# Query and key projection of a head pair as seven block products, spread expert slots and expert transposes

## The reference

```python
def sb_attend(q, k, v, q_pos, k_pos, bias):
    z = jnp.einsum('bqhe,bkhe->bhqk', q, k) * (HEAD_DIM ** -0.5) + bias
    mask = k_pos[None, :] < q_pos[:, None]
    log_beta = jax.nn.log_sigmoid(z)
    log_rest = jnp.where(mask, jax.nn.log_sigmoid(-z), 0.0)
    tail = lax.cumsum(log_rest, axis=3, reverse=True) - log_rest
    a = jnp.where(mask, jnp.exp(log_beta + tail), 0.0)
    return jnp.einsum('bhqk,bkhe->bqhe', a, v)

# layer 0
qkv = (rmsnorm(xp, g_attn[0]) @ w_qkv_a[0]).reshape(b, s, 3, N_HEADS_A, HEAD_DIM)
o_p = sb_prompt(qkv[:, :, 0], qkv[:, :, 1], qkv[:, :, 2], sb_bias[0])
xp = xp + o_p.reshape(b, s, -1) @ w_o_a[0]

def hmoe(h, ...):           # end of each layer; two experts a token, in one group
    a = jnp.einsum('td,edf->tef', h, w_g)
    u = jnp.einsum('td,edf->tef', h, w_u)
    return jnp.einsum('tef,efd->td', jax.nn.silu(a) * u * comb[:, :, None], w_d)
```

## Time and profile before

| what | before |
|---|---|
| median of 3 runs | 1375.42 us (1375.24 to 1375.64) |
| the profiled execution | 1374.61 us |
| its span | 1372.7 us |
| mean granted clock of TensorE in it | 0.987 |
| TensorE busy | 95% |
| VectorE, ScalarE, GpSimd busy | 46%, 24%, 33% |

### The profile page before, as it was taken

How to read it: one execution, slowest core, us unless ns; L and a number is a source line. 1 busy time by engine, 2 the same in 40 slices (tenths; PEclk the granted TensorE clock), 3 DMA queues, 4 the chain that set the end, 5 groups by cost and what they waited for, 6 DMA issues and landing times. The chain is left out here.

```text
span 1372.7 us, 20982 instructions
## 1 busy us (share of the span) xinstructions
PE 1297.9 (95%) x8732; PEld 919.7 (67%) x8732; DVE 637.2 (46%) x997; ACT 332.1 (24%) x667; POOL 451.9 (33%) x385
## 2 busy tenths in 40 slices
PE   8999999999999998899999999999998989999786
PEld 6787888545566764547868867877845656766453
DVE  3577675623622221164558558558436472121114
ACT  2222322302122221240115005005005312222112
POOL 2233444101011111005876576576450111111101
PEclk9999999999899999999999999999999999999998
DMA  8366534377699999971112012013050899999996
GB/s 312 135 219 220 194 106 174 101 309 299 246 418 418 419 418 420 412 289 51 57 56 94 12 55 94 11 56 96 9 139 2 330 353 419 417 419 419 419 417 259
DMA packets 92768, 318.83 MB, mean 232 GB/s; under 512 B 32969, under 2 KB 45401, under 8 KB 66564
## 3 DMA queue, kind: packets, MB, share of 16 engines
q1 hardware_dynamic: 77956, 279.95, 52.5%
q0 software_dynamic: 13536, 33.29, 6.7%
q10 hardware_dynamic: 1184, 4.26, 0.8%
HBM read 300.19 MB, written 33.28 MB: 243 GB/s over the span
## 5 line engine op out<-in xcount | busy, mean ns | idle before, releaser
L1941 PE MATMUL ps<-slots 128*128 128x384 f32 x768 | 262.0, 495 | 0.9 <-DVE vo L2240 0.6
L1941 PEld LDWEIGHTS ps<-slots 128*128 128x128 f32 x768 | 203.0, 270 | 43.7 <-issue 3.2
L1092 PE MATMUL ps<-slots,oT 128*64 128x256 f32 x1344 | 178.4, 390 | 23.3 <-DMA slots<-in_w_up 18.6
L581 PE MATMUL ps<-xnT_a,wA 128*128 128x260 f32 (+1 forms) x768 | 173.3, 386 | 1.7 <-DVE xnT_a L791 1.4
L1092 PEld LDWEIGHTS ps<-slots,oT 128*64 128x64 f32 x1344 | 121.4, 141 | 74.2 <-issue 26.2
L581 PEld LDWEIGHTS ps<-xnT_a,wA 128*128 128x128 f32 x768 | 145.6, 191 | 27.0 <-issue 5.8
L1604 POOL DMA_INDIRECT y_rows<-ysb,idx x30 | 30.2, 1007 | 361.1 <-DVE ysb L1127 361.1
L1118 DVE TENSOR_TENSOR sg<-sg,ps 64x256 f32<-64x256 f32 x64 | 26.5, 414 | 236.2 <-ACT sg L1115 236.2
L1127 DVE COPY ysb<-ps 64x512 f32<-64x512 f32 x60 | 41.6, 694 | 82.8 <-PE ps L1110 82.8
L1115 ACT ACTIVATE sg<-ps 64x256 f32<-64x256 f32 x64 | 24.4, 381 | 227.5 <-PE ps L1092 227.5
L2178 ACT ACTIVATE slots<-slots,neg 128x128 f32<-128x128 f32 (+1 forms) x192 | 64.1, 417 | 54.8 <-DVE neg L2285 49.3
(11 more groups left out here) (311 smaller groups left out, 2129.5 us busy)
## 6 DMA issues: line engine op xcount, KB each, us to landing
slots<-in_w_gate SPq DMA_DIRECT2D x42, 1024.0 KB, 23.2
slots<-in_w_up SPq DMA_DIRECT2D x42, 1024.0 KB, 26.6
slots<-in_w_down SPq DMA_DIRECT2D x36, 1024.0 KB, 26.1
slots<-in_unit_weights_b SPq DMA_DIRECT2D x12, 1536.0 KB, 7.1
wA<-in_qkv_pairs_a SPq DMA_DIRECT2D x24, 512.0 KB, 4.4
apart<-in_w_down SPq DMA_DIRECT2D x8, 1024.0 KB, 27.8
spare<-in_w_down SPq DMA_DIRECT2D x8, 1024.0 KB, 24.5
apart<-in_w_up SPq DMA_DIRECT2D x6, 1024.0 KB, 27.9
```

The costliest lines, as they stand in the source:

```text
L581: last = nc.tensor.matmul(bank(6 + h)[:, 0:half], wA[:, m, k, :], xnT[:, k, half * h:half * h + half], start=(k == 0), stop=(k == KT - 1))
L1092: last = nc.tensor.matmul(bank(q)[lo:lo + CAP, 0:FE], x[:, k, :], wt[:, k, :], start=(k == 0), stop=(k == KT - 1))
L1941: last = nc.tensor.matmul(bank(i % 2)[:, 0:UW], xT[:, kt, cols], wB[:, g, kt, :], start=(kt == 0), stop=(kt == KT - 1))
```

## The change

**Projection.** Write the 1024 inputs as two halves (weight tiles 0 to 3 and 4 to 7) and the 520 tokens as two halves of 260. Queries and keys of a pair for both token halves are a 2x2 block product of weights (q, k by input half) and tokens (input half by token half). It was eight block products of 4 matmuls; now it is seven, of sums and differences of blocks. GpSimd makes the mixed tokens once (`mix_tokens`, four operations on 1040 columns) and the mixed weights for every pair from 1 on (`mix_weights`, four on 512 columns). The mixed blocks live in `apart` and `wo_hi`, so the output weights 4 to 7 are loaded later. Three of the seven results are used more than once: ScalarE keeps product 1, VectorE adds what stands in the banks to it (`read`). Pair 0 is projected as before.

```diff
+        HK = KT // 2
+        NPROD, NREAD = 7, 5
+        mixed = flat(wo_hi)
...
+                def mixed_part(at, weights, tokens, start, stop):
+                    for k in range(HK):
+                        last = nc.tensor.matmul(bank(at)[:, 0:HALF], weights[:, k, :], tokens[:, k, :],
+                                                start=(start and k == 0), stop=(stop and k == HK - 1), skip_group_check=True)
+                    last.then_inc(s_mp, 1)
...
+                    pe.wait_ge(s_w[0], 16 * n + 16)
+                    pe.wait_ge(s_kve, 4 * n)
+                    mixed_part(7, q[:, 0:HK], x11, True, False)
+                    pe.wait_ge(s_mixw, 4 * n)
+                    pe.wait_ge(s_mixx, 4)
+                    mixed_part(6, mix_w[:, 1], mix_x[1], True, False)
+                    pe.wait_ge(s_ma, a + 1)
+                    mixed_part(7, q[:, HK:KT], x21, False, True)
+                    pe.wait_ge(s_md, d + 1)
+                    mixed_part(6, mix_w[:, 2], mix_x[2], False, False)
+                    pe.wait_ge(s_ma, a + 2)
+                    mixed_part(7, mix_w[:, 0], mix_x[0], True, False)
+                    pe.wait_ge(s_md, d + 2)
+                    pe.wait_ge(s_w[1], 16 * n + 16)
+                    mixed_part(6, kw[:, HK:KT], mix_x[3], False, True)
+                    pe.wait_ge(s_md, d + 3)
+                    mixed_part(7, mix_w[:, 3], x22, False, True)
...
+                def read(n, i, out, kept, at):
+                    dve.wait_ge(s_mp, NPROD * (n - 1) + (2, 4, 5, 6, 7)[i])
...
+                    nc.vector.tensor_tensor(out, kept, bank(at)[:, 0:HALF], ALU.add).then_inc(s_md, 1)
...
+                    nc.gpsimd.tensor_tensor(mix_w[:, 0], kw[:, 0:HK], kw[:, HK:KT], ALU.add).then_inc(s_mixw, 1)
+                    nc.gpsimd.tensor_tensor(mix_w[:, 2], q[:, 0:HK], kw[:, 0:HK], ALU.subtract).then_inc(s_mixw, 1)
...
                         if n < LAST:
-                            sp.wait_ge(s_proj, 6 * n + 2 * m + 2)
+                            if n and m < 2:
+                                sp.wait_ge(s_mixw, 4 * n)
+                                sp.wait_ge(s_mp, NPROD * (n - 1) + (3, 6)[m])
+                            else:
+                                sp.wait_ge(s_proj, in_plain(m, n, 1))
                             load_qkv(m, n + 1)
```

**Rows and transposes.** `iota64` now holds for slot c the place c // 4 + 16 (c mod 4), so the rows of an expert lie at every fourth slot first. The first transpose of a block and the first of each expert's hidden rows, which were products with the identity matrix, are now transposes like the others. Where further blocks are turned (`product`), nothing changes.

```diff
-    put("iota64", np.broadcast_to(np.arange(CAP), (128, CAP)))
+    slot = np.arange(CAP)
+    put("iota64", np.broadcast_to(slot // 4 + 16 * (slot % 4), (128, CAP)))
...
                     for i in range(HALFK):
-                        out, rows = bank(2 + half)[:, 128 * i:128 * i + 128], xs[w][:, HALFK * half + i:D:KT]
-                        if half == 0 and i == 0:
-                            last = nc.tensor.matmul(out, rows, ident, start=True, stop=True)
-                        else:
-                            last = nc.tensor.transpose(out, rows, ident)
+                        last = nc.tensor.transpose(bank(2 + half)[:, 128 * i:128 * i + 128], xs[w][:, HALFK * half + i:D:KT], ident)
...
-                        if product or f == 0:
+                        if product:
                             last = nc.tensor.matmul(out, cols, ident[0:CAP, 0:CAP], start=True, stop=True)
```

More of the change, by code:

```diff
@@ L426, in build, with in_plain @@
         LAST = NPAIR - 1
+        HK = KT // 2
+        NPROD, NREAD = 7, 5
+        mixed = flat(wo_hi)
+        mix_w = mixed[:, 0:4 * HK * 128].rearrange("p (i k c) -> p i k c", i=4, k=HK)
+        first_p, sum_16, sum_167 = [mixed[:, 4 * HK * 128 + HALF * i:4 * HK * 128 + HALF * (i + 1)] for i in range(3)]
+        mix_x = [flat(apart)[:, HK * HALF * i:HK * HALF * (i + 1)].rearrange("p (k m) -> p k m", k=HK) for i in range(3)]
+        mix_x.append(mixed[:, D * NPAIR // 2 - HK * HALF:].rearrange("p (k m) -> p k m", k=HK))
+        def in_plain(m, n, h):
+            return 2 * m + h + 1 if n == 0 else 6 + 2 * (n - 1) + h + 1
         with ExitStack() as ph, nc.Block() as block:
@@ L475, in build @@
                                  "srows_copied_act"))
+            early_sems = [s_mixx, s_mixw, s_mp, s_ma, s_md, s_qp, s_qr, s_qst, s_nb]
+            for early in early_sems:
+                live[-1].remove(early)
             s_w0, s_zero, s_tops = sem("sweights_cleared"), sem("zero_row"), sem("tables_read")
@@ L571, in project @@
                     half = SEQ // 2 if m == 0 else HALF
-                    for h in range(2):
+                    for h in halves:
+                        if n and h == 1:
+                            pe.wait_ge(s_md, NREAD * n)
                         if m == 0 and n == 0 and h == 1:
@@ L586, in turn_kv, with kv_place @@
+                def kv_place(c, n, t):
+                    o = 1536 + NZ if c == 0 and n and t == NT - 1 else 512 * 6 + 128 * t
+                    return ps[0:TILES[t][1], o:o + 128]
                 def turn_kv(c, n):
-                    pe.wait_ge(s_pev, 6 * n + 4 + 2 * c)
+                    if c == 0 and n:
+                        pe.wait_ge(s_md, NREAD * (n - 1) + 4)
+                    else:
+                        pe.wait_ge(s_pev, in_plain(1 + c, n, 1))
                     for t, rows in TILES:
-                        last = nc.tensor.transpose(ps[0:rows, 512 * 6 + 128 * t:512 * 6 + 128 * t + 128],
-                                                   qkvT[:, 1 + c, 128 * t:128 * t + rows], ident)
+                        last = nc.tensor.transpose(kv_place(c, n, t), qkvT[:, 1 + c, 128 * t:128 * t + rows], ident)
@@ L856, in _ @@
                         out_a.add(dve, 0, 1)
+                    else:
+                        read(n + 1, 0, sum_16, first_p, 6)
                     for h in range(2):
+                        if n < LAST and h == 1:
+                            early_keys(n + 1)
+                            late_queries(n + 1)
                         dve.wait_ge(s_msk, 4 * n + 2 * h + 2)
@@ L861, in _ @@
                             nc.vector.tensor_tensor_scan(P, P, keep[:, at:at + width][:, ::-1], 1.0, ALU.mult, ALU.add).then_inc(s_scan, 1)
+                            if n < LAST and h == 0 and lo == 0:
+                                read(n + 1, 1, sum_167, first_p, 6)
+                        if n < LAST and h == 0:
+                            late_keys(n + 1)
                         dve.wait_ge(s_scan, 4 * n + 2 * h + 2)
@@ L935, in next_keys, with mix_tokens, mix_weights @@
                             past(u + 3, 0)
+                def mix_tokens():
+                    b11, b12, b21, b22 = [xnT[:, HK * i:HK * i + HK, HALF * j:HALF * j + HALF] for i in range(2) for j in range(2)]
+                    for out, one, other, after in ((0, b12, b11, 0), (2, b22, b12, 0), (1, b22, mix_x[0], 1), (3, b21, mix_x[1], 3)):
+                        if after:
+                            pool.wait_ge(s_mixx, after)
+                        nc.gpsimd.tensor_tensor(mix_x[out], one, other, ALU.subtract).then_inc(s_mixx, 1)
+                def mix_weights(n):
+                    q, kw, done = wA[:, 0], wA[:, 1], 4 * (n - 1)
+                    pool.wait_ge(s_w[0], 16 * n + 16)
+                    pool.wait_ge(s_w[1], 16 * n + 16)
+                    if n > 1:
+                        pool.wait_ge(s_mp, NPROD * (n - 1))
+                    nc.gpsimd.tensor_tensor(mix_w[:, 0], kw[:, 0:HK], kw[:, HK:KT], ALU.add).then_inc(s_mixw, 1)
+                    nc.gpsimd.tensor_tensor(mix_w[:, 2], q[:, 0:HK], kw[:, 0:HK], ALU.subtract).then_inc(s_mixw, 1)
+                    pool.wait_ge(s_mixw, done + 1)
+                    nc.gpsimd.tensor_tensor(mix_w[:, 1], mix_w[:, 0], q[:, 0:HK], ALU.subtract).then_inc(s_mixw, 1)
+                    pool.wait_ge(s_mixw, done + 3)
+                    nc.gpsimd.tensor_tensor(mix_w[:, 3], q[:, HK:KT], mix_w[:, 1], ALU.subtract).then_inc(s_mixw, 1)
                 for u in range(3):
```

75 lines of the change are left out of this document (55 added, 20 removed).

## The result

| | before | changed kernel |
|---|---|---|
| median of 5 runs each, on one chip | 1375.42 us (1373.53 to 1378.64) | 1369.15 us (1368.44 to 1370.87) |
| ratio, 95% interval | | 0.9945 (0.9932 to 0.9959) |
| profiled execution, span | 1374.61, 1372.7 us | 1368.72, 1366.9 us |

The change is worth 6.3 us where I forecast 20, and the time lies outside my range (1350 to 1363). A second series of runs of the changed kernel gave 0.9949 (0.9929 to 0.9968).

A forecast was written before the change was run, and what follows sets the result against it. TensorE was taken to bound the attention stage, the expert weight stream the end of each expert stage. Terms -10.8 (projection), -7.5 (spread rows), -1.5 (transposes) sum to -19.8 us; forecast 1355 us, range 1350 to 1363.

The forecast's parts named there:

- Part 1, the products: Query and key projection of pairs 1 to 7: seven products for eight save 1.75 us a pair, 12.3 us.
- Part 1, the five reads and ScalarE's copies: VectorE's five PSUM reads a pair (0.45 us each) and ScalarE's copies meet due times by 0.5 to 1.7 us.
- Rival A: Head pairs: the hand-offs cost their bound, 8.4 us instead of 1.5, making 1362; chance 0.15.
- Part 1, the stalls booked at 1.5 us: Head pairs: all hand-off stalls together cost 1.5 us, bounds 0 and 8.4.
- The rule that I weighed: Head pairs: VectorE's product could wait a whole GpSimd addition, 1.1 us; TensorE loses 0.6 us a pair, making 1357.
- rival D: Head pairs: VectorE becomes the bound, 31.8 us a pair, making 1382; chance 0.04.
- Part 2: Expert stages: new slots for routed rows even the DMA engines, saving 4 us in layer 1, 3.5 in layer 0.
- rival B: Expert stages: spreading rows is worth nothing, as routed rows don't make the engines end apart; 1362.5, chance 0.13.
- The share's fall: Layer 1's expert weight stream: DMA share should fall from full to nothing within 8 us instead of 14.
- The prediction's other estimate: Expert stages, from the fullest DMA engine's routed rows: 4.7 and 5.3 us saved, 1352 in all.
- Part 3: Expert stages: identity products made transposes save 1.5 us, bounds -2.5 and +0.5.
- Rival C: Expert stages: transposes don't count as work for TensorE's clock, which falls to half in stretches; 1364, chance 0.06.

The follow-up runs named there:

- few mixes: Changed kernel with GpSimd's four weight mixes of pairs 2 to 7 cut to one element a partition each; 1359.45 us, 0.9879 of before.
- late mixes: Changed kernel with GpSimd's weight mixes held back until VectorE has made the second head's product; 1357.71 us, 0.9862 of before.
- VectorE's order changed: Changed kernel, value projection's second half split around the second head's weight transposes, VectorE's second past score behind the value copies; 1373.47 us, 0.9978 of before.
- slots alone: Kernel before with only the new slot order of routed rows; 1369.74 us, 0.9947 of before.
- transposes alone: Kernel before with only the expert stages' identity products made transposes; 1376.87 us, 1.0001 of before.
- both small parts: Kernel before with the new slot order and the expert transposes, projection as before; 1370.05 us, 0.9945 of before.
- the six gathers: Late mixes with the last six past-value gathers moved from pair 5's end to behind pair 6's masks; 1357.11 us, 0.9854 of before.

## Why the prediction was wrong

- **Part 1, the products: right.** 12.3 us of TensorE were to go. The loop without any stall takes 194.84 us, 207.25 - 194.84 = 12.41 us less.
- **Part 1, the five reads and ScalarE's copies: right.** All are in time, and the run with few mixes showed that they cost nothing. Rival A was right that 0.5 us was too little to spare, but of its six hand-offs only the product's failed, by more than A's bound.
- **Part 1, the stalls booked at 1.5 us: the step that failed.** I let the mixes start at 15 us and then charged them to the product alone, 2.20 for 1.49. They start at 14.6 us and lie beside the scans too, for which I took the undisturbed 2.86, though by my own times these ran to 15.7. The rows were in my hands: beside two masks the first head's scans took 3.72 and its product 2.20, 1.57 us more for both. That would have given 18.8 us for the weights and 1.1 us of wait a pair. Measured are scans 3.90 and product 2.38, which from 12.9 us give 19.2, and TensorE waits 1.47 us. Six times 1.47 is 8.8 us. Counted from the start of the matmuls before them to their own start, the transposes come 1.64 us later than with the late mixes, and each of the six pairs takes 1.68 us more (29.40 for 27.72, the first 30.24 for 28.54): 10.1 us. The longer pair 6 adds 3.4 (31.08 against 27.72), which no row of before could show. That is 13.5 us for the 1.5 booked. The 12.0 between them, less 0.1 that the products gave more, are the 11.9 that the loop lacks: 208.3 us where 207.25 - 10.8 = 196.45 was forecast.
- **The rule that I weighed was right, and I used it for one operation of two.** By the Trainium skill ("SBUF — State Buffer", "Who interferes with whom") a VectorE operation with two SBUF inputs and a GpSimd one that reads SBUF exclude each other for a whole instruction, and one with a single SBUF input, outside the two-port modes, doesn't contend. The trace bears out who: scans, product and past-score multiplication grew, copies from PSUM and reductions did not. It bears out the exclusion too, once the scans are read one by one. Of the same stretch of the changed kernel, the second scan alone:

```profile
94.34 1.70 DVE L960 TENSOR_TENSOR_SCAN slots<-slots,gain_rows 128x256 f32<-128x256 f32 x1
```

The long scan before it took its usual 2.28 us (92.14 to 94.42), with a GpSimd addition recorded from 93.83 to 95.48. From there the two engines take turns. The short scan, 0.67 us alone, ends 0.56 after that addition; the second addition, 1.27 alone, ends 1.06 after the scan (97.10); the product, 1.49 alone, ends 1.35 after the addition (98.45); the third addition ends 1.14 after the product (99.59). Each record begins while the other engine is at work and ends about its own length after the other's end, less 0.1 to 0.2 us: the added length is a wait until the other engine's operation is done. GpSimd's recorded times are the rougher ones, but VectorE's say the same. In the kernel with VectorE's order changed, two masks beside the long scan keep their 1.08 us each, and the scan that waits behind both takes 4.20 for 2.28. So the short scan let one addition by (1.03 us) and the product another (0.89). My sum allowed 0.7 us, all in the product, and even where I followed the rule I let one addition by, 0.6 us of wait a pair, where 1.47 came. And the "less than half of an addition's time" that I held against rival D is not what the earlier trace rows show: two masks of 1.07 us cost VectorE 1.57.
- **Part 2, 7.5 us: right in sum, less so in place, so in part luck.** 7.3 us measured alone. The share's fall within some 4 us is what was to show it, and rival B is out. But the last w_up came only 2.1 and 1.1 us earlier by the count that I had named (2.4 and 2.2 by the other), not 4 and 3.5, and the profile of the slots alone is 4.0 us shorter in the two expert stages, on which all 7.5 were forecast. It is also 0.7 and 1.2 us shorter in the stretches before and between them, which single profiles don't settle. The prediction's other estimate, 10 us in the stages, was further off. No trace here shows which engine moves which row.
- **Part 3, 1.5 us: too much.** Nothing in 12 runs (1.0001, interval 0.9987 to 1.0014, 1.8 us less to 1.9 more). TensorE's saved work turned into waits for weights.
- **Rival C:** the granted clock was 1.00 from 377 to 480 us, as before. From 1250 to 1335 it was 0.94 against 0.98, 0.98 with the transposes alone and 1.00 with both small parts, so no lower clock goes with the transposes. **Rival D:** not reached; with the late mixes VectorE keeps up with a pair of 27.72 us.
- **The sum with the mixes late is near the forecast's:** 0.9862 is 19.0 us (16.1 to 22.0), where 19.8 were forecast. The parts measured singly give 10.5 + 7.3 + 0 = 17.8, within the interval.

The kernel to use is the changed one with the line of **late mixes**: 0.9862 of before, 0.9% under the changed kernel. Moving the six gathers as well gave 0.9854, which isn't told apart from it.

## What to carry to other kernels

When work is given to an idle engine, lay it in time beside every operation of the other engine that it contends with, not only the one it was put next to. Count a whole operation of wait for each of them that it meets, and check that against a row in which both ran, read one record at a time: a row that merges several hides who waited for whom. Then ask which start time is free: the same four additions cost 8.8 us of TensorE's waits from the moment their data landed and none in those pairs when held back some 3 us, behind the product for which TensorE waits. And before an operation is moved on one engine, follow who waits for it: here a late past score held gathers, these held masks, and these the scans.

## What the runs showed of the hardware

- GpSimd's addition of two 128x512 float32 tiles takes 1.27 us alone and stands in the trace with 1.65 us when it begins beside one of VectorE's scans, 2.52 and 2.13 beside its product and its multiplication of two SBUF tiles. VectorE's records grow as well: short scan 0.67 to 1.70, product 1.49 to 2.38, multiplication 1.23 to 1.86 or 2.20. One engine's operation runs when the other's is done; neither is slowed while it runs. VectorE's copies from PSUM (1.49) and reductions (1.22) lost nothing beside the same additions.
- Eight gathers issued by GpSimd within 10 us, across the start of a head pair, went in five of nine profiles with a pause of ScalarE that names no engine (its copy 2.3 to 3.9 us late); with six of them moved there was none in three of three. The cause is open.
